# Second mixer: the convolution's pointwise product taken ahead of the second block of the output product

## The reference

```python
h = rms_norm_2(x, norm_g)
z = h @ w_in                                   # fox, convolution, NSA inputs and gates
o_a = fox_attention(...) * silu(f_gate)        # 256 columns
o_b = conformer_conv(glu_in, ...) * silu(c_gate)   # 256 columns
o_c = nsa_attention(...) * silu(n_gate)        # 512 columns
x = x + concatenate([o_a, o_b, o_c], -1) @ w_out   # 1024 x 1024

def conformer_conv(u, conv_w, conv_b, ln_g, ln_b, w_pw):
    y = causal depthwise convolution of 31 taps over glu(u), + conv_b
    yn = layer_norm(y) * ln_g + ln_b
    return silu(yn) @ w_pw                     # 256 x 256, the pointwise product
```

## Time and profile before

| | us |
|---|---|
| median of 3 runs | 1629.38 |
| lowest, highest | 1627.42, 1630.90 |
| the profiled execution, its own time | 1627.93 |
| its span | 1626.1 |
| granted TensorE clock, mean | 0.994 of full |
| PE busy, weight loads busy | 1592.5, 1368.9 |
| DVE, ACT, POOL busy | 951.4, 802.6, 167.1 |
| bytes read | 267 MB, at 165 GB/s |

### The profile page before, as it was taken

How to read it: one execution, slowest core, us unless ns; L and a number is a source line. 1 busy time by engine, 2 the same in 40 slices (tenths; PEclk the granted TensorE clock), 3 DMA queues, 4 the chain that set the end, 5 groups by cost and what they waited for, 6 DMA issues and landing times.

```text
span 1626.1 us, 22861 instructions
## 1 busy us (share of the span) xinstructions
PE 1592.5 (98%) x8768; PEld 1368.9 (84%) x8768; DVE 951.4 (59%) x1454; ACT 802.6 (49%) x1358; POOL 167.1 (10%) x187
## 2 busy tenths in 40 slices
PE   9999999999999999999999999999999989999997
PEld 7888899888888888888899988888888878878886
DVE  5555575444765555555456544665554778577865
ACT  6444465454364445444355454454443555453653
POOL 1000022211200000000022221120000301010100
PEclk9999999999999999999999999999999999999999
DMA  7665455443555554655546443446565453245421
GB/s 253 204 211 204 148 191 171 143 142 126 160 182 183 192 188 162 207 181 184 188 152 196 146 139 127 146 153 218 197 215 191 150 190 107 78 154 171 146 85 52
DMA packets 76718, 269.60 MB, mean 166 GB/s; under 512 B 8512, under 2 KB 9792, under 8 KB 76608
## 3 DMA queue, kind: packets, MB, share of 16 engines
q1 hardware_dynamic: 76320, 267.35, 49.4%
q10 hardware_dynamic: 288, 0.79, 0.1%
HBM read 267.06 MB, written 1.05 MB: 165 GB/s over the span
## 4 chain that ended last, share of the span: by engine, by line
PE 72%; DVE 5%; ACT 4%; issue 2%; POOL 1%; DMA 0%; POOLq 0%; DVEq 0%; ACTq 0%
PE bank L1433 20%; PE bank L1435 20%; PE bank L1434 20%; PE bank L1439 4%; PE bank L1558 2%; PE bank L1573 2%; DVE wlo L2281 1%; DVE cv L2278 1%; PE bank L1690 1%; ACT hh L1971 1%; ACT wk L2203 1%; PE bank L1500 1%; PE bank L1496 1%; PE bank L1492 1%; ACT whi L1968 1%
## 5 line engine op out<-in xcount | busy, mean ns | idle before, releaser
L2281 DVE TENSOR_TENSOR wlo<-raw,whi 128x1024 fp32r<-128x1024 f32 (+5 forms) x472 | 564.6, 1204 | 406.0 <-ACT whi L1968 370.4
L1968 ACT ACTIVATE whi<-raw 128x1024 fp32r<-128x1024 f32 (+4 forms) x500 | 508.9, 1029 | 426.4 <-PE bank L1435 394.6
L1433 PE MATMUL bank<-whi,hh 128*128 128x512 f32 (+3 forms) x1120 | 434.4, 388 | 0.0
L1435 PE MATMUL bank<-whi,hl 128*128 128x512 f32 (+3 forms) x1120 | 425.3, 380 | 0.0
L1434 PE MATMUL bank<-wlo,hh 128*128 128x512 f32 (+3 forms) x1120 | 424.8, 379 | 0.0
L1435 PEld LDWEIGHTS bank<-whi,hl 128*128 128x128 f32 x1120 | 210.5, 188 | 38.5
L1434 PEld LDWEIGHTS bank<-wlo,hh 128*128 128x128 f32 x1120 | 210.9, 188 | 35.9
L1433 PEld LDWEIGHTS bank<-whi,hh 128*128 128x128 f32 x1120 | 210.8, 188 | 35.6
L1433 PE MATMUL bank<-hh,whi 128*128 128x256 f32 x480 | 142.0, 296 | 0.0
L1433 PE MATMUL bank<-whi,gh 128*128 128x512 f32 x352 | 139.4, 396 | 0.0
L1435 PE MATMUL bank<-whi,gl 128*128 128x512 f32 x352 | 138.0, 392 | 0.0
(11 more groups left out here) (326 smaller groups left out, 1887.2 us busy)
## 6 DMA issues: line engine op xcount, KB each, us to landing
raw<-W SPq DMA_DIRECT2D x463, 512.0 KB, 3.3
raw<-W SPq DMA_DIRECT2D x26, 384.0 KB, 3.7
raw<-W SPq DMA_DIRECT2D x8, 416.0 KB, 3.0
tab<-tab SPq DMA_DIRECT2D x6, 384.0 KB, 4.0
raw<-W SPq DMA_DIRECT2D x4, 426.0 KB, 3.4
raw<-W SPq DMA_DIRECT2D x6, 192.0 KB, 2.6
x<-x_in SPq DMA_DIRECT2D x2, 512.0 KB, 6.5
tab<-gains SPq DMA_DIRECT2D x2, 512.0 KB, 4.9
```

What stands on the lines that cost most here:

```text
L1433: e.matmul(dst, ah, bh, start=start, stop=False)
L1435: return e.matmul(dst, al, bh, start=False, stop=stop)
L1968: return e.activation(dst, src, ACT.Copy)
L2281: return e.tensor_tensor(dst, src, hi.bitcast(F), ALU.subtract)
```

## The change

In the stream of weights of each second mixer the chunk "pw" moves from the third place behind the start of the output product to the second (ahead of the chunk of O1). The step waits for three blocks left instead of two, so for O0 alone, and says when it has been issued (`told.add("pw")`); `block_ready` holds O1 back until then.

```diff
-        rows("out", "w_out_2", l, OUT2[0:2], [(0, 1024)], 1)
+        rows("out", "w_out_2", l, OUT2[0:1], [(0, 1024)], 1)
         rows("pw", "conv_pw_2", l, range(2), [(0, 256)], 2)
-        rows("out", "w_out_2", l, OUT2[2:], [(0, 1024)], 1)
+        rows("out", "w_out_2", l, OUT2[1:], [(0, 1024)], 1)
...
-            yield from until(lambda: len(blocks) <= 2)
+            yield from until(lambda: len(blocks) <= 3)
             c = self.next("pw")
+            told.add("pw")
...
+        def block_ready():
+            return mixed[OUT2[4 - len(blocks)]] and (len(blocks) == 4 or "pw" in told)
+
...
-            if not main_left[0] and owed[0] >= 1.2 and blocks and mixed[OUT2[4 - len(blocks)]]:
+            if not main_left[0] and owed[0] >= 1.2 and blocks and block_ready():
...
-            if mixed[OUT2[4 - len(blocks)]]:
+            if block_ready():
```

## The result

| | before | after |
|---|---|---|
| median, lowest to highest, us | 1627.44 (1627.31 to 1630.90, 8 runs) | 1623.38 (1622.75 to 1624.15, 8 runs) |
| the profiled execution, its span | 1627.93, 1626.1 | 1622.75, 1620.9 |
| PE busy, mean clock | 1592.5, 0.994 | 1589.0, 0.995 |

The changed kernel is faster by 0.3%: ratio 0.997, 95% interval 0.9961 to 0.9979. That is 4.9 us with an interval of 3.4 to 6.3; the medians differ by 4.1. Forecast were 1624.7 us and a gain of 4.7, from the median of the 3 runs known then, 1629.38.

A forecast was written before the change was run, and what follows sets the result against it. PE, busy 98% of the span, was taken as the bound. Per layer 2.18 - 1.02 - 0.35 = 0.81 us from order plus 1.54 from the clock, 2.35; over two layers 1629.38 - 4.7 = 1624.7 us, range 1621.8 to 1629.2.

The forecast's parts named there:

- The exchanged chunks: Third chunk's low part on DVE grows to 1024 columns and delays rgn and O0: cost 0.35 us a layer.
- PE up to the new wait: From O0 on PE: transposes kc,wk come 3.71 us later, as before; the pointwise product starts after another 0.44 us.
- The new wait: PE ahead of vbd,cw waits for DVE's convolution gate to free bank 6: cost 1.02 us a layer.
- The old wait: PE's 2.18 us loss ahead of transposes kc,oc disappears; DVE's NSA gate ends 0.5 us ahead of PE.
- The clock: PE stays at 2.4 GHz across O2 and O3, taking 5.70 us instead of 7.24: gain 1.54 us a layer.
- Behind it: From O4 on, no queue is late and the gain is carried on: 2.35 us a layer, 4.7 in all.
- (B): Rival: only the order pays, the clock gives nothing back at O2 and O3; 1627.8 us, chance 0.27.
- (C): Rival: NSA gate late again behind two low parts, PE waits 0.7 us at the old place; 1626.1 us, chance 0.09.
- (D): Rival: clock falls behind both thin places, at bank 6 and at 1424; 0.73 us a layer slower, 1630.8, chance 0.08.

The follow-up runs named there:

- e4: Changed kernel with the low part of the third chunk made 12 us later on DVE, behind the silu: 1621.28 us (5 runs).
- e5: Changed kernel with the pointwise product written into bank 3 instead of bank 6: 1621.60 us (6 runs), ratio 0.9967.
- e3: Kernel before, with only the first token tile's NSA gate issued two steps earlier on DVE, ahead of the convolution's gate: 1622.08 us (5 runs), ratio 0.9968.
- e2: Kernel before, with 8 unread matmuls of 512 columns put on PE ahead of the waiting transposes kc,oc: 1625.88 us (11 runs), ratio 0.9986.
- e6: Changed kernel with the edits of e3 and e5 together (bank 3, NSA gate earlier): 1621.66 us (5 runs), ratio 0.9962.
- e7: Changed kernel with the edits of e3, e5 and e4 together: 1620.81 us (5 runs), ratio 0.9962.
- e1: The changed kernel measured again, nothing edited: 1622.08 us (6 runs) beside 1628.22 of the kernel before, ratio 0.9966.
- e8 to e10: Kernel before, unchanged, three more profiled executions: 1627.34, 1626.25 and 1627.38 us.

## Why the prediction was right

1. *The exchanged chunks*, 0.35 us. Measured 0.35 (9.02 to 9.37), undone by e4.
2. *PE up to the new wait.* O0 to the transposes kc,wk 3.71 us, as forecast.
3. *The new wait*, 0.7 to 0.9 us idle and 1.02 in all forecast. Measured 0.78 idle; from the old 13.55 to 12.37 the order gained 1.18 behind O0, against 2.18 - 1.02 = 1.16. e5 shows that it is for bank 6. Its length was built from the start and end of rows that already existed. That it fits to 0.02 us is in part luck, for two small misses cancel: the product starts 0.36 us behind the transposes kc,wk (1417.67 to 1418.03) instead of 0.44, and the gate 1.69 behind the product's start (1418.03 to 1419.72) instead of 1.62.
4. *The old wait.* Gone, with 0.63 us to spare where 0.5 was forecast; e3 shows its cause, and e5 that the slack was as thin as that.
5. *The clock*, 1.54 us. Measured 7.24 to 5.70, and e2 shows it alone.
6. *Behind it.* Nothing was given back: O4 comes 2.37 and 2.41 us earlier, 4.8 in all for 4.7 forecast.

The absolute time, 1624.7, was less sure than the gain: the median that I started from, 1629.38, lay 1.9 above that of all 8 runs. The same gain from 1627.44 would give 1622.7; measured is 1623.38.

Of the rivals, (B) had too much of a chance. What spoke for it was a wait of 1.92 us elsewhere, at 1504 to 1512, that left the clock up. All twelve traces have that wait, of 1.88 to 2.06 us. Behind it the clock stays up in the four of the kernel before and in e2 to e4, e6 and e7, and falls in both of the changed kernel and in e5, there behind 1.92 us. So the length of a wait alone does not tell. The free-running window that the Trainium skill tells of ("TensorE: Matmul & The Clock Gate", "Part 1: The HAM clock gate") agrees with 1562, where the clock is down in one execution of the kernel before and up in three; behind the 2.00 us wait the fall did not come and go. Why not, no run here settles: what PE does around these waits differs, and was not varied.

(C) came within 0.63 us of happening, and happens in e5. (D) did not occur: in every trace from e1 to e7 the clock is 1.00 from 1414 to 1426. One reading in (D) was wrong. The stretch 1388 to 1393 does not have only narrow matmuls, most of its time goes to matmuls of 512 columns; the narrow ones (24 of 32 columns, 1385.70 to 1388.29) stand ahead of it in the trace of before, and in e3 the clock stays up there. A term that I did not have is the rest, stretches that differ between executions: 1.4 us between the layers for the profiled pair, 1.0 the other way in the opening. The median of 8 runs moved by 4.1 where the distances say 4.8.

## What to carry to other kernels

When a matrix engine waits for an instruction whose inputs were long ready, look at what stands ahead of it in its own engine's order; moving that one instruction (e3) gave as much as moving a product and its weights. Here a wait of 2 us cost another 1.5 behind it through the clock, so the price of a wait is read from both sides. Where whole runs spread by more than the term in question, measure from an instruction that the edit doesn't reach to one behind it: terms of 0.3 us showed to 0.02.

## What the runs showed of the hardware

Eight matmuls whose result nobody reads, put into a wait on PE, made the kernel 2.3 us faster (e2). At this place the clock stayed at 2.4 GHz behind waits of 0.78 or 0.79 us (six, in two executions of the changed kernel and in e4) and fell to 1.2 GHz behind waits of 1.99 or 2.00 us in all eight.

A fall does not cost the same everywhere. From O4 of the first layer to ACT's second rgn of the next, the four traces without a fall (e6, e8 to e10) take 143.09 to 143.41 us, and the three with one at about 1508 (the changed kernel, e1, e5), where PE waits for other engines, 143.14 to 143.30: nothing lost. The five with one at about 1562 (before, e2 to e4, e7), where PE is never idle, take 144.72 to 146.36. No run set such a fall on purpose; this is what the twelve traces have in common.
